# Modulation weights laid out by output, multiplied once on GpSimd and summed on ScalarE between heads; latent attention's values taken by four heads

## The reference

```python
mod = c @ w_ada[l] + b_ada[l]          # c: [1, 1024], w_ada[l]: [1024, 3072]
shift, scale, gate = jnp.split(mod, 3, axis=-1)
h = _layer_norm(x, LN_EPS) * (1.0 + scale[:, None, :]) + shift[:, None, :]
```

```python
p = jax.nn.softmax(s, axis=-1).astype(v.dtype)
return jnp.einsum('bhqk,bkhd->bqhd', p, v)
```

## Time and profile before

| | |
|---|---|
| median of 3 runs | 2605.05 us |
| the profiled execution's own time | 2613.94 us |
| its span in the profile | 2612.1 us |
| TensorE's granted clock over the span | 0.983 of full speed |
| busy: TensorE, GpSimd, VectorE, ScalarE | 97%, 74%, 43%, 26% |
| branch B's attention, first layer | about 169 to 212.7 us of the span |
| latent projections | 212.7 to 229.2 us |
| branch A's attention, first layer | 229.2 to 295.6 us |
| `ada` on GpSimd, first layer | 169.4 to 291.4 us, with two pauses |

### The profile page before, as it was taken

One profiled execution on the slowest core, in us unless ns is written; L12 is line 12 of the kernel. 1 busy time (PEld: TensorE's weight loads), 2 busy tenths in 40 slices (PEclk: granted clock), 3 DMA queues, 4 the chain that ended last, 5 costly groups with the idle time before them and its releaser, 6 DMA issues.

```text
span 2612.1 us, 38097 instructions
## 1 busy us (share of the span) xinstructions
PE 2524.0 (97%) x13034; PEld 2019.4 (77%) x13034; DVE 1116.2 (43%) x1618; ACT 684.1 (26%) x1300; POOL 1936.3 (74%) x1567
## 2 busy tenths in 40 slices
PE   7999999999999999999999999999999999999998
PEld 6776777777788888777687777788887777778776
DVE  5556443224222225546625224322225338650775
ACT  3445233112201012536314111210002115231341
POOL 6777855989889898867873899898998573447704
PEclk9999999999999999999999999999999999989998
DMA  4233421233233323223420223333332121112201
GB/s 136 86 97 98 154 73 53 86 92 99 90 98 96 97 93 92 89 89 96 163 89 29 92 87 99 95 97 96 97 96 93 57 81 57 41 35 89 75 23 64
DMA packets 67569, 226.62 MB, mean 87 GB/s; under 512 B 7552, under 2 KB 16256, under 8 KB 66944
## 3 DMA queue, kind: packets, MB, share of 16 engines
q1 hardware_dynamic: 66016, 221.32, 26.8%
q10 hardware_dynamic: 1440, 3.79, 0.4%
HBM read 222.99 MB, written 2.10 MB: 86 GB/s over the span
## 4 chain that ended last, share of the span: by engine, by line
POOL 36%; PE 32%; issue 20%; DVE 5%; DMA 3%; POOLq 2%; ACT 0%; SPq 0%; DVEq 0%; ACTq 0%
POOL whi L469 18%; POOL wlo L472 12%; PE ps L565 8%; PE ps L567 8%; PE ps L566 8%; POOL raw L488 3%; POOL ada_acc L490 3%; DMA raw<-w_gate 2%; DMA raw<-w_abc 1%; PE ps L674 1%; PE ps L643 1%; PE ps L599 1%; PE ps L953 1%; DVE q_parts L1883 1%; POOLq L471 1%
## 5 line engine op out<-in xcount | busy, mean ns | idle before, releaser
L469 POOL TENSOR_TENSOR whi<-raw,one 128x512 fp32r<-128x512 f32 (+3 forms) x732 | 794.5, 1085 | 546.7 <-PE ps L567 471.6
L472 POOL TENSOR_TENSOR wlo<-raw,whi 128x512 fp32r<-128x512 f32 (+3 forms) x732 | 952.9, 1302 | 57.3
L565 PE MATMUL ps<-h,whi 128*128 128x512 f32 x1984 | 795.7, 401 | 34.5 <-POOL wlo L472 16.5
L567 PE MATMUL ps<-h,wlo 128*128 128x512 f32 x1984 | 780.6, 393 | 0.0
L566 PE MATMUL ps<-h,whi 128*128 128x512 f32 x1984 | 780.3, 393 | 0.0
L565 PEld LDWEIGHTS ps<-h,whi 128*128 128x128 f32 x1984 | 376.7, 190 | 137.2 <-POOL wlo L472 29.7
L567 PEld LDWEIGHTS ps<-h,wlo 128*128 128x128 f32 x1984 | 376.0, 190 | 81.9
L566 PEld LDWEIGHTS ps<-h,whi 128*128 128x128 f32 x1984 | 376.6, 190 | 79.2 <-issue 2.4
L565 PE MATMUL ps<-y,whi 128*128 128x512 f32 x640 | 250.9, 392 | 0.6 <-DVE y L1805 0.6
L567 PE MATMUL ps<-y,wlo 128*128 128x512 f32 x640 | 249.0, 389 | 0.0
L566 PE MATMUL ps<-y,whi 128*128 128x512 f32 x640 | 249.0, 389 | 0.0
(11 more groups left out here) (286 smaller groups left out, 3012.3 us busy)
## 6 DMA issues: line engine op xcount, KB each, us to landing
raw<-w SPq DMA_DIRECT2D x120, 512.0 KB, 3.4
raw<-w_abc SPq DMA_DIRECT2D x68, 512.0 KB, 3.5
raw<-w_ada SPq DMA_DIRECT2D x48, 512.0 KB, 3.5
raw<-w_gate SPq DMA_DIRECT2D x48, 512.0 KB, 3.5
raw<-w_in SPq DMA_DIRECT2D x44, 512.0 KB, 3.5
raw<-w_pac SPq DMA_DIRECT2D x16, 512.0 KB, 3.5
raw<-w_o SPq DMA_DIRECT2D x16, 512.0 KB, 3.5
raw<-w_out SPq DMA_DIRECT2D x16, 512.0 KB, 3.5
```

The lines of the kernel that those rows point to most:

```text
L469: pool.tensor_tensor(whi[:, s, r], raw[:, s, r], one[:, 0:1].to_broadcast([P, cols // 2]), ALU.mult).then_inc(hi_made, 1)
L472: pool.tensor_tensor(wlo[:, s, r], raw[:, s, r], whi[:, s, r].bitcast(F32), ALU.subtract).then_inc(made, 1)
L565: nc.tensor.matmul(out, whi[:, s, w], moving[:, c, :], start=(c == 0), stop=False)
L567: last = nc.tensor.matmul(out, wlo[:, s, w], moving[:, c, :], start=False, stop=(c == n - 1))
```

## The change

1. The host lays `w_ada` out by output: unit m now has 128 outputs on partitions and all 1024 inputs along the free dimension. `c` is one tile `c_all` of 128 x 1024, the same row on every partition, loaded anew by SyncE in each layer (512 KB, just ahead of the first `w_ada` load).
2. GpSimd does one multiplication per unit, in place, with the full tile `c_all` as second operand. The adds are gone.
3. ScalarE sums each unit along the free dimension: a Copy over 128 x 1024 in place with `accum_out`, a column of `modsum`. It does so between heads. In branch B the sums of units 0 to 7 stand in steps i = 3, 5, ... 17. In branch A those of units 8 to 23 stand in steps i = 0, 1, 3, 4, 6, 7, ... 21, 22, each behind the exponential of head i + 2. The sum now raises `ada_used[s]`, on which the slot's next load waits. ScalarE waits in its own queue for the multiplication (`ada_made`).
4. TensorE's `ada_sums` and its wait `mod_got` are gone. VectorE adds `b_ada` to `modsum`.
5. Branch A takes the values by groups of four heads: at steps i = 3, 7, 11, ... the two pairs follow each other, a fourth slot `pt_a` is added, and the reciprocals of a block are made one step earlier, by the exponential of its last head.

```diff
-        ada_acc = at("ada_acc", [P, 3, UNIT], y_at + Y_C[0] * TILE)
+        c_all = at("c_all", [P, D], y_at + Y_C[0] * TILE)
+        slots_a = [*tmp, at("pt_a", [P, T], y_at + 12 * TILE)[:]]
...
                 sp.dma_start(rope[:], d["rope_b"]).then_inc(in_rope, 16)
+                sp.dma_start(c_all[:], d["c_all"]).then_inc(in_c, 16)
...
-            def ada(thirds):
-
-                for third in thirds:
-                    acc = ada_acc[:, third, :]
-                    if third == 2:
-                        pool.wait_ge(s_done, s_n.now() + NQB * B_HEADS)
-                    for c in range(DC):
-                        s = c % 2
-                        factor = cvec[:, c:c + 1].to_broadcast([P, UNIT])
-                        pool.wait_ge(landed[s], land_n[s].next(16))
-                        if c == 0:
-                            pool.tensor_tensor(acc, raw[:, s, :], factor, ALU.mult).then_inc(ada_used[s], 1)
-                        else:
-                            pool.tensor_tensor(raw[:, s, :], raw[:, s, :], factor, ALU.mult).then_inc(ada_step, 1)
-                            pool.wait_ge(ada_step, step_n.next())
-                            pool.tensor_tensor(acc, acc, raw[:, s, :], ALU.add).then_inc(ada_used[s], 1)
+            def ada(first, n):
+
+                for m in range(first, first + n):
+                    s = m % 2
+                    pool.wait_ge(landed[s], land_n[s].next(16))
+                    pool.tensor_tensor(raw[:, s, :], raw[:, s, :], c_all[:], ALU.mult).then_inc(ada_made, 1)
...
-                ada((0,))
+                pool.wait_ge(in_c, ic_n.next(16))
+                ada(0, DC)
                 cut(0)
-                ada((1, 2))
-                s_n.next(80)
+                ada(DC, 2 * DC)
                 pairs(6)
...
+                evicted = (0,) if group == 2 else (2, 3)
...
-                    elif chunks <= 4 and i >= 2 and i % 2 == 0:
+                    elif chunks <= 4 and i >= 2 and i % group in evicted:
                         pe.wait_ge(pt_ready, pt_0 + i - 1)
...
-                    if hh == n_heads - 2:
+                    if hh == n_heads - group:
                         reciprocals(qb)
+                    pe.wait_ge(pt_ready, pt_0 + i + 2)
...
-                    if i >= 2 and i % 2 == 0:
+                    if group == 2 and i >= 2 and i % 2 == 0:
                         values(i - 2)
+                    elif group == 4 and i % 4 == 3:
+                        values(i - 3)
+                        values(i - 1)
...
-                def ada_sums(third):
-
-                    for s in range(2):
-                        pe.wait_ge(ada_used[s], ada_0[s] + 4 * (third + 1))
-                    for m in range(third * DC, (third + 1) * DC):
-                        last = nc.tensor.matmul(ps[3][:, m:m + 1], ada_acc[:, third, m % DC * P:(m % DC + 1) * P], ones,
-                                                start=True, stop=True)
-                    if third == 2:
-                        last.then_inc(ada_done, 1)
...
-                v_units(C_TILES // 2, C_VSTART, (6, 7), outputs=y_n.now(), fill=ada_sums)
+                v_units(C_TILES // 2, C_VSTART, (6, 7), outputs=y_n.now())
...
-                pe.wait_ge(mod_got, mod_n.next())
...
                     if i + ahead < n:
                         expo(i + ahead)
-                    if i > 0 and i % n_heads == 0:
+                    if aside:
+                        aside(i)
+                    if (i > 0 and i % n_heads == 0) if group == 2 else (i < n and i % n_heads == n_heads - 1):
                         r_n.next()
...
+                def ada_sum(m):
+
+                    act.wait_ge(ada_made, am_n.next())
+                    nc.scalar.activation(raw[:, m % 2, :], raw[:, m % 2, :], ACT.Copy,
+                                         accum_out=modsum[:, m:m + 1]).then_inc(ada_used[m % 2], 1)
+
+                def ada_in_b(i):
+                    if i >= 3 and i % 2 and i < 3 + 2 * DC:
+                        ada_sum((i - 3) // 2)
+
+                def ada_in_a(i):
+                    if i % 3 < 2 and i < 3 * DC:
+                        ada_sum(DC + i // 3 * 2 + i % 3)
...
-                    if block_end:
-                        dve.wait_ge(p_ready, p_0 + i)
-                        nc.vector.reciprocal(rden[:, 0:n_heads], den[:, qb % 2, 0:n_heads]).then_inc(rden_ready, 1)
+                    last = i if group == 4 else i - 1
+                    if 0 <= last < n and last % n_heads == n_heads - 1:
+                        dve.wait_ge(p_ready, p_0 + last + 1)
+                        nc.vector.reciprocal(rden[:, 0:n_heads], den[:, last // n_heads % 2, 0:n_heads]).then_inc(rden_ready, 1)
...
-                dve.wait_ge(ada_done, adone_n.next())
-                nc.vector.tensor_tensor(mod_all[:, bass.ds(lay, 1), :], ps[3][:, 0:ADA_UNITS].unsqueeze(1),
-                                        v2_all[:, bass.ds(lay, 1), 0:ADA_UNITS], ALU.add).then_inc(mod_got, 1)
+                for s in range(2):
+                    dve.wait_ge(ada_used[s], au_n[s].next(ADA_UNITS // 2))
+                nc.vector.tensor_tensor(mod_all[:, bass.ds(lay, 1), :], modsum[:].unsqueeze(1),
+                                        v2_all[:, bass.ds(lay, 1), 0:ADA_UNITS], ALU.add)
...
-        w_ada=a["w_ada_2"].reshape(DEPTH, DC, P, 3, D).transpose(0, 3, 1, 2, 4).reshape(DEPTH, ADA_UNITS, P, D), w_in2=units(a["w_in_2"], in2),
+        w_ada=a["w_ada_2"].reshape(DEPTH, D, ADA_UNITS, P).transpose(0, 2, 3, 1), w_in2=units(a["w_in_2"], in2),
```

More of the change, by code:

```diff
@@ L177, in build @@
         y = at("y", [P, 20, T], y_at, F32R)
-        ada_acc = at("ada_acc", [P, 3, UNIT], y_at + Y_C[0] * TILE)
+        c_all = at("c_all", [P, D], y_at + Y_C[0] * TILE)
+        sqa = [at(f"sqa{u}", [P, T], y_at + (Y_C[0] + u) * TILE) for u in range(3)]
         places = [y_at + i * TILE for i in range(16, 20)] + [hd + i * TILE for i in (18, 19, 8, 9, 10, 11, 12)]
@@ L215, in build @@
         qg8 = own("qg8", [P, 1])
-        cvec = own("cvec", [P, DC])
+        modsum = own("modsum", [P, ADA_UNITS])
         mod_all = own("mod_all", [P, DEPTH, ADA_UNITS])
@@ L302, in build @@
         mg_ready = sem("mg_ready")
-        mod_got = sem("mod_got")
         mod_ready = sem("mod_ready")
@@ L506, in _ @@
                                       (done_n[0], UNITS_1[0]), (done_n[1], UNITS_1[1]),
-                                      (hi_n, 2 * sum(UNITS_1)), (step_n, 3 * (DC - 1)), (s_n, 80)]):
+                                      (hi_n, 2 * sum(UNITS_1)), (ic_n, 16)]):
                 pairs(B_TILES + 1)
@@ L620, in attention @@
             def attention(n_heads, scores, value, chunks, ring, slots, banks, o_banks, r_bank, o_read=None, between=None,
-                          ready=None):
+                          group=2, ready=None):
                 n = NQB * n_heads
@@ L722, in _, with v_units @@
                 pe.wait_ge(bank_free[0], free_n[0].now() + 1)
-                token_sums(sqa[0:2])
-                token_sums(sqa[2:3], bank=7).then_inc(nsum_done, 1)
+                token_sums([q[:] for q in sqa[0:2]])
+                token_sums([sqa[2][:]], bank=7).then_inc(nsum_done, 1)
                 fin_n.next(2 * B_TILES)
-                def v_units(pairs_of_v, starts, banks, outputs=None, fill=lambda k: None):
+                def v_units(pairs_of_v, starts, banks, outputs=None):
                     def turn_v(s):
@@ L856, in full_values @@
                     return lambda qb, hh, c: v[:, c, col(hh):col(hh) + HD]
-                attention(A_HEADS, a_scores, full_values(va_, lambda hh: hh * HD), NQB, ring_3, tmp, (2, 3, 4), (7, 1), 5,
-                          o_read=y_ready, between=a_values_read)
+                attention(A_HEADS, a_scores, full_values(va_, lambda hh: hh * HD), NQB, ring_3, slots_a, (2, 3, 4), (7, 1), 5,
+                          group=4, o_read=y_ready, between=a_values_read)
                 unit(0, DC, h_hi, h_lo)
@@ L865, in _ @@
                 rb_n.next()
-                def ada_sums(third):
-                    for s in range(2):
-                        pe.wait_ge(ada_used[s], ada_0[s] + 4 * (third + 1))
-                    for m in range(third * DC, (third + 1) * DC):
-                        last = nc.tensor.matmul(ps[3][:, m:m + 1], ada_acc[:, third, m % DC * P:(m % DC + 1) * P], ones,
-                                                start=True, stop=True)
-                    if third == 2:
-                        last.then_inc(ada_done, 1)
-                ada_0 = [n.now() for n in ada_n]
-                for n in ada_n:
-                    n.next(12)
-                v_units(C_TILES // 2, C_VSTART, (6, 7), outputs=y_n.now(), fill=ada_sums)
+                v_units(C_TILES // 2, C_VSTART, (6, 7), outputs=y_n.now())
                 pairs(2, DC, h_hi, h_lo)
@@ L1150, in next_input, with attention @@
                     gained(c, gain)
```

(13 more changed lines are left out.)

42 lines of the change are left out of this document (19 added, 23 removed).

## The result

The change makes the kernel slower: 2615.18 us, median of 19 runs (2607.92 to 2620.30), against 2606.60 us for the kernel before in the same comparison (19 runs, 2601.91 to 2612.74). The ratio is 1.0031, with a 95% interval of 1.0023 to 1.0039, or +6 to +10 us. The forecast of 2613.6 us was 8.6 us above the median that it knew; 8.6 us were measured.

What follows compares the result with a forecast made beforehand. TensorE, busy 97% of the span, was taken as the bound. Per layer, +7.7 (branch A's ring) - 3.57 (`ada_sums`) + 0.2 (branch B) = +4.3 us; two layers +8.6 on 2605.05 gave 2613.6 us, range 2601 to 2626.

Steps and rivals of the forecast that it cites:

- The ring: Branch A: a slot's loop of load, multiply, wait and sum paces the first 22 steps; branch ends 7.7 us later.
- T: Branch A: one slot's loop for two units, from load through multiply to sum, 7.5 us against TensorE's 5.7 us.
- "Nothing" for the end of branch B: End of branch B: its last sum waits for its unit until about 216 us, delaying nothing that matters; no cost.
- Branch B: Branch B's attention: eight ScalarE sums mostly hidden, +0.2 us a layer, bounds 0 and 2.
- `ada_sums`: TensorE's modulation sums, three times a layer: removing them gains 3.57 us a layer.
- Values by four: Branch A: groups of four heads save 1.2 us of switches and 1.3 us of end waits a layer.
- switches: Branch A, TensorE switching to values and back: 8 of 16 fall away at 0.15 us, 1.2 us a layer.
- tail waits: End of branch A: two TensorE waits, 0.35 and 0.97 us, go because reciprocals come a step earlier; 1.3 us.
- The sum: Whole kernel: +7.7 - 3.57 + 0.2 = +4.3 us a layer, +8.6 us for two layers, giving 2613.6 us.
- The first: Branch A rival: multiply costs 1.89 us, T near 7.0; +0.8 us a layer, 2606.6 us; chance 0.22.
- The second: Branch A rival: the slot's loop keeps up with TensorE, only gains stay, 2593.3 us; chance 0.12.
- The third: Branch A rival: TensorE's clock falls because of its pauses, +12 us a layer more, near 2638 us; chance 0.08.

Runs made afterwards that it cites:

- e5: Changed kernel with GpSimd's multiply taking the first column of `c_all` as a broadcast operand instead of the full tile; 2607.3 us, ratio 0.9998 against before.
- e3: Changed kernel with branch A's 16 sums at every second step instead of two in three; 2606.15 us, ratio 0.9995 against before.
- e4: Changed kernel, but in branch A the multiply frees the slot and ScalarE's sums read `x`, waiting for nobody; 2596.54 us, ratio 0.9964 against before.
- e6: Changed kernel with branch B's last sum (unit 7) behind ScalarE's last output copy instead of ahead of it; 2613.11 us, ratio 1.0014 against before.
- e2: Changed kernel with values by pairs and three slots again, the moved `pt_ready` wait kept; 2618.77 us, ratio 1.0048 against before.
- e1: Kernel before plus only branch A's values by four and the `pt_ready` wait moved in every attention; 2600.99 us, ratio 0.9984 against before.
- e7: Changed kernel with units 8 to 23's products in separate buffers, branch A's sums every second step, unit 7's sum behind the output copy; 2594.7 us, ratio 0.9947 against before.

## Why the prediction was right, step by step

**The ring: right, its T 0.16 us too large.** Forecast T = 7.5 us, measured 7.34. The branch's end was forecast 7.7 us later; latents and A together are 7.5 and 7.0 us longer. In the first layer, counted from the first `turn`, seven loops took 1.1 us less than forecast, but the first sum ended 0.2 us later and the tail behind the sum of unit 22 took 16.2 us (284.56 to 300.74) instead of 15.5: two errors that nearly cancel. The multiply was forecast at 2.36 us and measured 2.36. Two full tiles take 113.5 / 48, and the multiply costs what the add did. Here the trace agrees with the Trainium skill, GPSIMD Engine Reference, section 3.1, whose one figure for a two-input `tensor_tensor`, about 2.6 cycles an element, makes no difference between them; with the broadcast form of e5, 1.89 us, it doesn't. The sum was forecast at 1.17 us to the end of its reading and measured 1.15 (239.52 to 240.67). So nearly all of the 0.16 us lies in the way from the release to the next multiply, 3.64 to 3.94 us and 3.78 on average over the seven loops, forecast as 3.85 "with some slow loads", and in the semaphores, 0.05 instead of 0.1. e3, e4 and e5 took the loop's cause apart: more steps for it, no wait in it, a shorter part of it.

**"Nothing" for the end of branch B: right in the sum, with a step left out.** The prediction says "behind it stand only an output copy and copies of the latent projections, whose first starts at 217: nothing". It counted ScalarE's work behind the last sum, but not who waits for the output copy. The timelines of ScalarE, VectorE and TensorE in the kernel after:

```profile
211.92 1.06 ACT L1251 ACTIVATE raw<-raw 128x1024 f32<-128x1024 f32 x1 [1.70 <-POOL raw L481]
...
212.97 0.65 ACT L1166 ACTIVATE y<-rdens 128x256 fp32r<-128x256 f32 x1
```

```profile
213.65 0.62 DVE L1550 TENSOR_TENSOR y<-rdens,y 128x256 fp32r<-128x256 f32 x1 [2.62 <-ACT y L1166]
```

```profile
225.03 0.47 PE L788 MATMUL ps<-whi,c_hi 128*128 128x512 f32 x1 [0.69 <-DVE qa L1696]
```

ScalarE waits for GpSimd, the copy of `y` for ScalarE, and VectorE's subtraction for the copy; so VectorE reaches the rotations of `qa` later, which TensorE needs before it can go on. In e6 the chain is gone and the latents are at 16.5, but the time isn't: the first `turn` of branch A waits for ScalarE's copies and first exponential in any case. That a late `qa` costs nothing was therefore luck, with 0.9 us to spare: in e2's first layer it was later still, and 1.1 us got through.

**Branch B: right in sum, wrong in parts.** +0.2 was forecast and +0.3 measured. But e1, with no sums in B, has 42.8 us there: the sums cost 0.9, and 0.6 were gained by a part of the diff to which the prediction gave no price. The wait for `pt_ready` now stands behind the reciprocals in every attention, so that TensorE spreads the reciprocals while the last copy is under way: before, it waits 1.14 us for that copy ahead of the last spread, and in e1 0.37 us behind it. The 0.5 us gained in branch C's attention, which the forecast lacks, are put down to the same line because nothing else of e1's edit touches that stage; no run has the line alone.

**`ada_sums`: right.** C1 falls by 3.70 us a layer, forecast 3.57; no L872 is left, and TensorE's busy time falls by 13 us in all.

**Values by four: near in size, its parts less so.** 2.5 us were forecast, 1.2 of switches and 1.3 of tail waits; where TensorE sets the pace it is 2.1 (e4 and e7, latents and A together against before). "Nothing new waits" was wrong: the two tail waits of 0.35 and 0.97 us went, but the last `turn` now waits 0.72 us for its exponential. That leaves 0.6 for the tail and, as the rest, 1.5 for the eight switches. The qualification "only where TensorE sets the pace" was right and too short: with GpSimd at 57.8 of 61 us the pace passes to GpSimd after 1 us (e1). And in the changed kernel, where the ring sets the pace, the prediction let only the tail count (3.5 us of reciprocals, tail waits and switches taken together), while e2 against after gives A alone 2.0 and 2.4 us more.

**The sum.** By the stages: forecast +4.3 us a layer, measured +3.6 and +3.1. Latents and A together came out 0.2 and 0.7 us under the +7.7, C1 brought 0.1 and C2 0.5 more than forecast, and B took 0.1 more. That the median hit to a tenth is luck within an interval of 4 us, and so is part of the stages' agreement, since their errors have both signs.

**The rivals.** The first is e5: with 1.89 us the loss is gone, as its price said, but the multiply doesn't cost 1.89. The second, a loop that keeps up, needs what e4 and e7 build. The prediction priced it at 11.8 us under the kernel before, 5.9 a layer; e4 is 9.8 and e7 14.3 us under theirs by the medians, and by the stages both are 6.0 us a layer. The third, the lower clock, was seen in one of the two layers of the kernel after. Windows of branch A in the kernel after:

```profile
243.00:248.00 5.00, 4.16 (x20) 2.66 (x22) 2.22 (x4) 2.76 (x9) 3.35 (x2) 0.57 0.45 159
248.00:253.00 5.00, 5.00 (x48) 4.30 (x45) 0.86 (x2) 2.81 (x7) 2.68 (x2) 0.75 0.49 158
253.00:306.00 53.00, 48.56 (x394) 32.76 (x392) 35.57 (x57) 29.59 (x69) 33.41 (x20) 1.00 0.53 185
```

In the first layer TensorE was at its lower level of 1.2 GHz for most of 243 to 248 us and half of the next five, behind its waits that end at 241.39 and 243.84, and then came back. In the second layer the clock was 1.00 from the start of the branch to its end. The two layers differ by only 0.45 us in A (78.46 and 78.01): so what the clock took was, all but that, time in which TensorE would have waited for the ring.

## What to carry to other kernels

Before an engine joins the work that frees a buffer, work out the whole loop (load, each engine's work, each wait in a queue) for one buffer and set it against the pace of the consumer; busy shares don't show it, and here ScalarE was busy for 59% of the stage and still stopped TensorE. Free the buffer at the earliest reader, by writing the product elsewhere, and let the engine that has time do the waiting: an in-order queue with critical work in it should not wait for a side job. Where a stage table shows a loss, look whether the next stage gives it back: the latents' 1.0 us did not exist past the first `turn`. Time freed on an engine that nobody waits for brings nothing by itself, but it can be what lets the next change count.

## What the runs showed of the hardware beside this

- A two-input elementwise operation of GpSimd over 128 x 1024 takes 2.36 us with two full tiles and 1.89 us with one operand broadcast along the free dimension, with the same multiply in both (the kernel after and e5).
- ScalarE's Copy with accumulation of 128 x 1024 from SBUF takes 1.06 us, and the reading of the accumulator 0.19 us more, overlapping by some 0.1 us.
- "To B" has two values, 40.8 and 42.4 us, in different layers and executions of like code: before has the low one twice, after the high one twice, e1 one of each, e6 one of each in the other order. The windows of e1, first layer and second:

```profile
131.00:139.00 8.00, 8.00 (x30) 6.23 (x30) 4.92 (x8) 4.01 (x8) 2.34 (x2) 0.79 0.01 2
1121.00:1129.00 8.00, 8.00 (x22) 6.05 (x22) 5.34 (x9) 4.32 (x8) 0.81 (x1) 0.57 0.01 2
```

  TensorE is busy without a break in both and does 30 matmuls in one and 22 in the other. After a wait of 1.74 us ahead of this stretch, the same in both, the granted clock is at the lower level (1.2 GHz) and comes back sooner in one (0.79 over the 8 us) than in the other (0.57). This accounts for a difference of 1.5 us in a single profile, within one execution of one kernel, so no edit needs to be behind it. What decides between the two was not tried.
